# Inverting the delta rule's triangular matrices: transposes by VectorE in squares of 32 rows, the last level on one quadrant, three masks by GpSimd

## The reference

```python
kb = k * beta[..., None]
a = jnp.where(strict, jnp.einsum('bhntd,bhnsd->bhnts', kb, k) * decay, 0.0)
eye = jnp.eye(c, dtype=q.dtype)
t_inv = lax.linalg.triangular_solve(a + eye, jnp.broadcast_to(eye, a.shape),
                                    left_side=True, lower=True, unit_diagonal=True)
u = jnp.einsum('bhnts,bhnsv->bhntv', t_inv, v * beta[..., None])
...
def step(state, inp):
    v_new = u_n - jnp.einsum('bhtd,bhdv->bhtv', w_n, state)
    o = jnp.einsum('bhtd,bhdv->bhtv', qg_n, state) + jnp.einsum('bhts,bhsv->bhtv', qk_n, v_new)
    state = state * gl_n[..., None, None] + jnp.einsum('bhsd,bhsv->bhdv', kd_n, v_new)
```

## Time and profile before

| | |
|---|---|
| median of 3 runs | 3351.74 us (3351.55 to 3360.6) |
| profiled execution, its own time | 3355.1 us |
| its span | 3353.2 us |
| PE, PEld busy in the span | 3059.8 us (91%), 2534.2 us (76%) |
| DVE, ACT, POOL busy | 1617.2 us (48%), 1181.0 us (35%), 479.8 us (14%) |
| first run of the delta stage | from 153.8 us to 338.7 us |
| second run of the delta stage | first DVE tile at 1345.3 us, last one ends at 1529.5 us |

### The profile page before, as it was taken

One profiled execution on the slowest core, in us unless ns is written; L12 is line 12 of the kernel. 1 busy time (PEld: TensorE's weight loads), 2 busy tenths in 40 slices (PEclk: granted clock), 3 DMA queues, 4 the chain that ended last, 5 costly groups with the idle time before them and its releaser, 6 DMA issues. The chain is left out here.

```text
span 3353.2 us, 40954 instructions
## 1 busy us (share of the span) xinstructions
PE 3059.8 (91%) x15744; PEld 2534.2 (76%) x15744; DVE 1617.2 (48%) x2106; ACT 1181.0 (35%) x1647; POOL 479.8 (14%) x279
## 2 busy tenths in 40 slices
PE   6899899886999989898998978999898999969899
PEld 5799888775887867898887856887676767758787
DVE  4566547533554345565476334553475552233233
ACT  3543543323222234334543232222333652232222
POOL 2332003001000022330030000000162223110000
PEclk9999999998999999999999988999999999989999
DMA  4100300322222231002103222222431222223122
GB/s 148 51 1 1 100 26 20 101 76 78 87 92 72 92 102 49 26 1 75 50 1 101 76 75 88 92 83 82 122 82 49 71 63 79 66 75 98 65 95 93
DMA packets 264333, 235.11 MB, mean 70 GB/s; under 512 B 23188, under 2 KB 247938, under 8 KB 263554
## 3 DMA queue, kind: packets, MB, share of 16 engines
q1 hardware_dynamic: 264194, 233.20, 23.0%
HBM read 226.88 MB, written 6.29 MB: 70 GB/s over the span
## 5 line engine op out<-in xcount | busy, mean ns | idle before, releaser
L120 PE MATMUL PS<-HHI,WHI 128*128 128x512 f32 x2016 | 805.4, 399 | 93.3 <-DVE WLO L172 70.5
L121 PE MATMUL PS<-HLO,WHI 128*128 128x512 f32 x2016 | 797.2, 395 | 0.0
L122 PE MATMUL PS<-HHI,WLO 128*128 128x512 f32 x2016 | 796.6, 395 | 0.0
L172 DVE TENSOR_TENSOR WLO<-RAW,WHI 128x1024 fp32r<-128x1024 f32 (+2 forms) x212 | 361.6, 1707 | 513.8 <-ACT WHI L168 512.7
L168 ACT CAST WHI<-RAW 128x1024 fp32r<-128x1024 f32 (+2 forms) x212 | 304.1, 1437 | 744.3 <-PE PS L122 611.8
L120 PEld LDWEIGHTS PS<-HHI,WHI 128*128 128x128 f32 x2016 | 382.7, 190 | 194.1 <-issue 78.5
L122 PEld LDWEIGHTS PS<-HHI,WLO 128*128 128x128 f32 x2016 | 382.2, 190 | 87.8
L121 PEld LDWEIGHTS PS<-HLO,WHI 128*128 128x128 f32 x2016 | 382.9, 190 | 86.7 <-issue 2.0
L120 PE MATMUL PS<-SH,WHI 128*128 128x512 f32 x800 | 316.9, 396 | 45.1 <-DVE SL L379 45.1
L121 PE MATMUL PS<-SL,WHI 128*128 128x512 f32 x800 | 315.5, 394 | 0.0
L122 PE MATMUL PS<-SH,WLO 128*128 128x512 f32 x800 | 315.5, 394 | 0.0
(11 more groups left out here) (427 smaller groups left out, 4490.6 us busy)
## 6 DMA issues: line engine op xcount, KB each, us to landing
RAW<-in_w_up SPq DMA_DIRECT2D x44, 1024.0 KB, 5.1
RAW<-in_w_in SPq DMA_DIRECT2D x82, 512.0 KB, 4.1
RAW<-in_w_down SPq DMA_DIRECT2D x44, 512.0 KB, 3.3
RAW<-in_w_in SPq DMA_DIRECT2D x20, 1024.0 KB, 5.4
RAW<-in_w_gate SPq DMA_DIRECT2D x32, 512.0 KB, 4.0
RAW<-in_w_mlp SPq DMA_DIRECT2D x16, 1024.0 KB, 5.4
RAW<-in_w_mlp SPq DMA_DIRECT2D x32, 512.0 KB, 3.5
RAW<-in_w_out SPq DMA_DIRECT2D x24, 512.0 KB, 3.5
```

Source lines behind the costliest of these rows:

```text
L120: e.matmul(out, wh, xh, start=first and n == 0, stop=False)
L121: e.matmul(out, wh, xl, start=False, stop=False)
L122: last = e.matmul(out, wl, xh, start=False, stop=final and n == len(quads) - 1)
L172: self.lo_st.done(dve.tensor_tensor(self.lo[:, s], self.raw[:, s], self.hi[:, s], ALU.subtract), f"unit{s}")
```

## The change

The inverse is computed in the same levels, with these differences.

- The transposes of `T` after levels 0 to 4 are made by DVE, one instruction for the four heads of a lane, which transposes each square of 32 x 32 elements in its place. `T` holds nothing outside blocks of 32 rows until level 5. No copy by ACT belongs to them. The transpose ahead of level 6 stays on TensorE with its copy by ACT.
- Level 6 multiplies only one quadrant: 64 x 64 elements of `AT` without a mask, 64 x 64 of `T` and `TT`. ACT's copy and DVE's subtraction are cut to the same quadrant.
- The masks of levels 1, 2 and 4 are made by POOL; those of 0, 3 and 5 stay on DVE. `LB` has two buffers for each lane, used by turns. One kind of semaphore, `lbe`, is added for each lane.
- The scaling of `AT` by beta moves from POOL to ACT, where it is four instructions, one for each head.

```diff
+        B[d]["LB"] = new(f"LB{d}", [P, 2, 4, P])
+        FIRST, SECOND = (slice(0, 64), slice(64, P)), (slice(64, P), slice(0, 64))
...
+                def level_mask(m, n):                                 # POOL
+                    for d in lanes:
+                        if n == 1:
+                            pool.wait_ge(S["atb"][d], m + 1)
+                            if m:
+                                pool.wait_ge(S["p"][d], m * L)
+                        elif n == 2:
+                            pool.wait_ge(S["tt0"][d], m + 1)
+                        else:
+                            pool.wait_ge(S["p"][d], m * L + n - 2)
+                        pool.tensor_tensor(B[d]["LB"][:, n % 2], B[d]["AT"][:, :, :], heads(C[:, PAIR + d * LEVELS + n, :], 4), ALU.mult).then_inc(S["lbe"][d], 1)
...
-                    for d in lanes:
-                        b = B[d]
-                        pool.wait_ge(S["at"][d], m + 1)
-                        pool.tensor_tensor(b["AT"][:, :, :], b["AT"][:, :, :], wide(beta_of(chunk(m, d), d), P), ALU.mult).then_inc(S["atb"][d], 1)
+                    level_mask(m, 1)
+                    level_mask(m, 2)
                     for d in lanes:
                         if m + 1 < CH:
                             broadcast_g(m + 1, d)
+                    level_mask(m, 4)
...
                 def level_p(m, d, n):                                 # PE
-                    pe.wait_ge(S["lb"][d], m * LEVELS + n + 1)
+                    if n in (3, 5):
+                        pe.wait_ge(S["lb"][d], m * 3 + (n + 1) // 2)
+                    elif n < L:
+                        pe.wait_ge(S["lbe"][d], m * 3 + n // 2 + 1)
...
+                            last = pe.matmul(hb(d, 0, h)[two, one], B[d]["AT"][one, h, two], B[d]["T"][one, h, one], start=True, stop=True)
...
-                            last = pe.matmul(hb(d, 1, h), b["PP"][:, h, :], b["TT"][:, h, :], start=True, stop=True)
+                            last = pe.matmul(hb(d, 1, h)[one, two], b["PP"][two, h, one], b["TT"][two, h, two], start=True, stop=True)
...
                             for d in lanes:
-                                turn(m, d, n - 1)
+                                if n == L:
+                                    turn(m, d, n - 1)
                                 level_p(m, d, n)
...
+                        for d in lanes:                               # ACT, after the four exponentials of each lane
+                            b = B[d]
+                            act.wait_ge(S["at"][d], m + 1)
+                            for h in H4:
+                                last = act.activation(b["AT"][:, h, :], b["AT"][:, h, :], ACT.Copy, scale=BETA[:, chunk(m, d), 4 * d + h:4 * d + h + 1])
+                            last.then_inc(S["atb"][d], 1)
...
+                def turn(m, d, n):                                    # DVE
+                    src, dst = ("T", "TT") if n else ("TT", "T")
+                    flat = lambda name: B[d][name][:, :, :].rearrange("p h n -> p (h n)")
+                    dve.wait_ge(S["t"][d], m * (L - 1) + n) if n else dve.wait_ge(S["tt0"][d], m + 1)
+                    dve.transpose(flat(dst), flat(src)).then_inc(S["tc"][d], 1)
...
                                     dve.tensor_tensor(b["T"][:, :, :], b["T"][:, :, :], per_head(bank(d, 1)), ALU.subtract).then_inc(S["t"][d], 1)
-                                    level_mask(m, d, n + 1)
+                                    if n + 1 in (3, 5):
+                                        level_mask(m, d, n + 1)
+                                    if n < L - 1:
+                                        turn(m, d, n)
```

More of the change, by code:

```diff
@@ L695, in delta_stage @@
     B = [{n: new(f"{n}{d}", [P, 4, P]) for n in
-          ("GB", "EG", "DM", "AT", "LB", "T", "TT", "PP", "QK", "QG", "KG", "KD", "ST", "SD")} for d in lanes]
+          ("GB", "EG", "DM", "AT", "T", "TT", "PP", "QK", "QG", "KG", "KD", "ST", "SD")} for d in lanes]
     for d in lanes:
@@ L793, in turn @@
                 def turn(m, d, n):
[L794 to L798, removed]
+                    pe.wait_ge(S["t"][d], m * (L - 1) + n)
                     for h in H4:
-                        last = pe.transpose(hb(d, 1, h), src[:, h, :], C[:, IDENT, :])
+                        last = pe.transpose(hb(d, 1, h), B[d]["T"][:, h, :], C[:, IDENT, :])
                     last.then_inc(S["tr"][d], 1)
                 def level_p(m, d, n):
-                    pe.wait_ge(S["lb"][d], m * LEVELS + n + 1)
+                    if n in (3, 5):
+                        pe.wait_ge(S["lb"][d], m * 3 + (n + 1) // 2)
+                    elif n < L:
+                        pe.wait_ge(S["lbe"][d], m * 3 + n // 2 + 1)
                     if n == 1:
@@ L812, in level_p @@
                         pe.wait_ge(S["pc"][d], m * L + n - 1)
+                    one, two = FIRST[d], SECOND[d]
                     for h in H4:
-                        last = pe.matmul(hb(d, 0, h), B[d]["LB"][:, h, :], B[d]["T"][:, h, :], start=True, stop=True)
+                        if n < L:
+                            last = pe.matmul(hb(d, 0, h), B[d]["LB"][:, n % 2, h, :], B[d]["T"][:, h, :], start=True, stop=True)
+                        else:
+                            last = pe.matmul(hb(d, 0, h)[two, one], B[d]["AT"][one, h, two], B[d]["T"][one, h, one], start=True, stop=True)
                     last.then_inc(S["p"][d], 1)
                 def level_d(m, d, n):
-                    b = B[d]
+                    b, one, two = B[d], FIRST[d], SECOND[d]
                     pe.wait_ge(S["pc"][d], m * L + n)
@@ L927, in _ @@
                                 b = B[d]
[L928 to L931, removed]
+                                if n == L:
+                                    act.wait_ge(S["tr"][d], m + 1)
+                                    act.copy(b["TT"][:, :, :], per_head(bank(d, 1))).then_inc(S["tc"][d], 1)
                                 act.wait_ge(S["p"][d], m * L + n)
-                                act.copy(b["PP"][:, :, :], per_head(bank(d, 0))).then_inc(S["pc"][d], 1)
+                                rows, cols = (slice(0, P), slice(0, P)) if n < L else (SECOND[d], FIRST[d])
+                                act.copy(quarter(b["PP"], rows, cols), quarter(per_head(bank(d, 0)), rows, cols)).then_inc(S["pc"][d], 1)
             @block.vector
@@ L945, in level_mask @@
                     b = B[d]
-                    if n:
-                        dve.wait_ge(S["p"][d], m * L + n - 1) if n > 1 else dve.wait_ge(S["tt0"][d], m + 1)
-                    else:
+                    if n == 0:
                         dve.wait_ge(S["atb"][d], m + 1)
-                        if m:
-                            dve.wait_ge(S["p"][d], m * L)
-                    dve.tensor_tensor(b["LB"][:, :, :], b["AT"][:, :, :], heads(C[:, PAIR + d * LEVELS + n, :], 4), ALU.mult).then_inc(S["lb"][d], 1)
+                    if n == 0 and m:
+                        dve.wait_ge(S["p"][d], m * L)
+                    if n > 1:
+                        dve.wait_ge(S["p"][d], m * L + n - 2)
+                    dve.tensor_tensor(b["LB"][:, n % 2], b["AT"][:, :, :], heads(C[:, PAIR + d * LEVELS + n, :], 4), ALU.mult).then_inc(S["lb"][d], 1)
+                def turn(m, d, n):
[3 more added lines that the diff above has]
+                    dve.transpose(flat(dst), flat(src)).then_inc(S["tc"][d], 1)
                 for m in range(CH + 1):
@@ L982, in _ @@
                             level_mask(m, d, 0)
[L983 to L985 removed]
+                            dve.wait_ge(S["lb"][d], m * 3 + 1)
+                            dve.tensor_tensor(b["TT"][:, :, :], heads(C[:, IDENT, :], 4), b["LB"][:, 0], ALU.subtract).then_inc(S["tt0"][d], 1)
+                            turn(m, d, 0)
                     if m:
```

8 lines of the change are left out of this document (4 added, 4 removed).

## The result

The median went from 3354.18 to 3333.67 us (5 runs each, side by side; 3351.55 to 3360.6 and 3331.75 to 3339.54), a ratio of 0.994 with a 95% interval of 0.992 to 0.995. A second comparison gave 0.993 (0.991 to 0.995). The forecast was 3328, faster, and the time lies in its range. The profiled execution took 3331.8 us against 3355.1, so 23.3 us less; that is the difference explained here.

What follows compares the result with a forecast made beforehand. The prediction took PE's issue to bound the levels, at 4.44 of 4.76 us. Gains of 1.4 + 1.1 + 0.5 = 3.0 us a chunk, four chunks, two layers, 24 us, gave 3328 us, range 3306 to 3355.

Steps and rivals of the forecast that it cites:

- The transpose's price: A DVE transpose of 128 x 512 was taken at 0.69 us, with the next instruction 0.60 behind.
- rival C: DVE's float32 transpose is slow, deciding from 1.19 us on; at 2.0 us each, 3390 us in all; chance 9%.
- (a): After levels 1 and 3 (transpose, no mask): interval of 3.92 us instead of 4.76, twice a chunk.
- (b): After levels 2 and 4 (mask, then transpose): DVE replaces PE as the bound; intervals 6.48 and 5.6 us.
- (c): From level 5 to level 6, with PE's transpose and the quadrant's groups: 4.01 us (3.61 to 4.49).
- The base: D of level 1 to D of level 6 before the change: 25.33 us, set against 23.9 after; gain 1.4.
- (d): Ahead of level 1, DVE's line decides: first D at 256.9 instead of 257.99, gain 1.1 us a chunk.
- (e): Behind level 6, the two D groups are 0.24 us shorter each: gain 0.5 us a chunk.
- The clock: PE's granted clock was expected to stay at 1.00 in the levels, with PE above 85% busy.
- A: More gain: POOL and DVE rarely meet after level 2 (5.12 us), quadrant groups cost 0.45; 3311 us; chance 18%.
- B: Waiting takes PE's place: slowed masks give 7.24 after level 2, 6.5 after level 4; quadrant 0.89; 3352 us; chance 13%.
- D: PE's clock falls to the lower level in the levels, since it waits more: 95 us slower, 3447; chance 2%.

## Why the prediction was right

**The transpose's price.** Taken 0.69 and 0.60, measured 0.71 and 0.63: right, and rival C fell with it.

**(a) After levels 1 and 3: 3.92 forecast, 4.17 measured.** The chain was right. Its term "transpose of lane 0 at 0.60" was too small: it starts at 0.72, so lane 1's subtraction comes at 1.35 instead of 1.20. Another 0.08 is from P1 to D0, 0.97 for 0.89. In the first chunks the interval after level 1 was about 5.0, with D at the lower clock. Moving the transposes out from between the subtractions took it to 3.79.

**(b) After level 2: 6.48 forecast, 5.9 to 7.9 measured (mean 7.0).** This is the step that failed most. The mechanism was right, DVE as the bound, with masks that meet POOL: 5.9 in the first chunk, where one mask of the two meets it, 7.25 in the fourth, where the second takes 1.78, and light products on POOL brought it to 5.23. The size was short: the term of 1.28 a mask, where the masks took 1.56 to 1.59 us in the second chunk, and a clock's dip came on top. After level 4, 5.6 forecast and 5.41 measured: PE's issue, as said.

**(c) 4.01 forecast, 4.17 measured.** PE issues without a wait. The quadrant's groups start 0.52 to 0.61 apart (taken 0.65), but each transpose group ahead of one takes 0.58 instead of 0.44. The Trainium skill ("TensorEngine Tiling (Array Packing)", Key Properties) says that a change of the tiling mode drains TensorE. If it is in those 0.14 us, the drain costs a fraction of what the upper bound of 0.89 allowed. One comparison bears on it: with the transposes back on TensorE, such a group behind D takes 0.49 ahead of a full P (215.73 to 216.22) and 0.58 ahead of a quadrant's. So 0.09 us goes with the quadrant; that it is the drain is not shown.

**The base.** The forecast set 25.33 us of the fourth chunk against its sum. Over all eight chunks the stretch averages 25.79 before, so 3.7 us of gain were left out (the fourth chunk meets neither a slow mask after level 1, as the second with 5.55 and the third with 5.12, nor the second layer's slow clock, 6.10); the levels then missed by 202.7 - 191.2 = 11.5 us. Their gain was 3.6, not 11.2.

**(d) Gain ahead of level 1: 1.1 a chunk forecast, 2.0 to 2.9 measured in chunks 2 to 4.** The terms for the collisions on DVE were too large here. Masks and identities took 0.70, 1.64, 1.23 and 0.69 us, where 1.28, 1.41, 1.66 and 1.41 were put. Lane 0's mask met POOL only for its first 0.15 us, and POOL's mask of level 2 for lane 1 waits for that lane's subtraction from the identity, so POOL stands while DVE makes it (247.79). The same rule of meetings thus took 0.5 us a chunk in (b) and gave 1.4 in (d), and nothing in the forecast told the two apart. The traces do. Each of the 34 masks and identities over 0.72 us in the changed kernel ended 0.55 us (545 to 551 ns) after the end of the POOL instruction that was running when it started. The row of before fits: POOL's `QG` ends at 215.26 and DVE's mask at 215.80. So what a meeting costs is the rest of POOL's instruction, and the start of the mask sets it, not one price for all. The first chunk of the first layer lost 0.3 us, with both P groups at the lower clock. That of the second layer gained 1.4, because before the change it was the one at the lower clock.

**(e) 0.5 forecast and measured.** What was overlooked is that the quadrant also does away with a mask.

**The clock.** "it stayed at 1.00 in a stretch where PE was busy for 3.24 of 6 us, and I see it above 85% busy" was wrong after level 2, where PE is busy for 3.13 and 3.14 of 6 us. After such a stretch the clock fell in the second chunk of each stage (1.5 us) and stayed at 1.00 in the third. It was wrong in the first chunk too, with 0.50 from 165 to 168 us, but the kernel before has that as well (0.51 over the same stretch). Nothing here separates the stretches that are followed by a fall from those that are not.

**The rivals.** A asked for few meetings after level 2 (5.12) and quadrant groups at 0.45: neither came true. Few meetings came ahead of level 1, where A had not put them. B's 7.24 after level 2 came true in the fourth chunk of each stage, its slow mask after level 4 in none. C fell by the transpose's row. D happened in parts of two levels of each stage, for some 5 us in all instead of 95.

The parts don't add up. Taken back alone, the transposes, the masks, the quadrant and the scaling cost 13, 21, 18 and 3 us by the ratios, 55 in all, and together they bring 21. Each part alone lets another engine bound the level: DVE at 5.22 us without the masks' move, PE at 4.55 without the transposes'. The clock is in these sums too: 4 to 5 of the 21 us, most of 3 of the 18 and all of the 3 are TensorE at its lower clock.

## What to carry to other kernels

When an edit moves the bound from the engine that issues the products to the one that prepares them, look at what stands between a result and its consumer on the new one: taking the masks out from there gave 14 us, and moving the transposes out from between the two lanes' subtractions 3 to 5 more. A cost that an experiment shows in the total need not be where the theory puts it: the doubled transposes hit their sum with 35 on the path instead of 48, and the lower clock made up the rest. A contended instruction is cheap where the engine has slack and dear in the chain, so place it before asking for its duration. A forecast that is right in its sum should still be checked term by term, as here two terms were off by 7 to 8 us in opposite directions.

## What the runs showed of the hardware

- DVE's transpose of 128 x 512 float32 takes 694 to 712 ns in all 64 cases from `T` to `TT`, also beside POOL at work. A mask or a subtraction from the identity, with two SBUF inputs, took 668 to 1781; the 24 of 64 that met no instruction of POOL took at most 693, and POOL's own mask 1266 to 1768. A slowed one ended 545 to 551 ns after the POOL instruction that it had found at work, in all 34 cases. The Trainium skill ("GPSIMD Engine Reference", Key points) has the contention for DVE's instructions with two SBUF inputs; the trace agrees, by these rows.
- A DVE instruction that reads the result of the one before started 0.68 to 0.73 us after it, another 0.57 to 0.64 (where the one before was not slowed by POOL).
- PE's group of four products that starts after a pause holds the next one back by 0.97 us (253.50 to 254.46), one that follows without a pause by 0.89.
